# Stick-breaking attention's steps two units apart, and its sums in two rounded passes in layer 1

## The reference

```python
z = jnp.einsum('bhqd,bhkd->bhqk', qb, k).astype(jnp.float32) * scale
log_1mb = jnp.where(mask, jax.nn.log_sigmoid(-z), 0.0)
later = lax.cumsum(log_1mb, axis=3, reverse=True) - log_1mb
w = jnp.where(mask, jnp.exp(jax.nn.log_sigmoid(z) + later), 0.0)
return jnp.einsum('bhqk,bhkd->bhqd', w.astype(v.dtype), v)
```

## Time and profile before

| | |
|---|---|
| median of 3 runs | 1025.94 us (1024.55 to 1026.02) |
| the profiled execution | 1024.67 us, its span 1023.0 us |
| mean granted TensorE clock | 0.997 |
| TensorE matmuls | 985.5 us busy (96%) |
| VectorE | 764.5 us (75%) |
| ScalarE | 549.9 us (54%) |
| GpSimd | 47.3 us (5%) |
| HBM | 176.67 MB read, 176 GB/s over the span |

### The profile page before, as it was taken

The page is one execution under the profiler, slowest core; times in us unless marked ns, Lnnn a source line. Parts: engine busy times, 40 slices in busy tenths (PEclk is TensorE's granted clock), DMA queues, the critical chain, the costliest instruction groups (busy, mean ns, idle before and its releaser), DMA issues. The chain is left out here.

```text
span 1023.0 us, 17644 instructions
## 1 busy us (share of the span) xinstructions
PE 985.5 (96%) x6784; PEld 872.3 (85%) x6784; DVE 764.5 (75%) x1185; ACT 549.9 (54%) x843; POOL 47.3 (5%) x104
## 2 busy tenths in 40 slices
PE   6999999999999999999999999999999999999996
PEld 6877889999897888888889778999988878888885
DVE  5988997878765866879765669887887567656665
ACT  7455426475755645544463663545656565444543
POOL 5004000000000004000000110000000000000000
PEclk9999999999999999999999999999999999999999
DMA  9797438466654666686657853565565546666652
GB/s 339 230 191 179 125 103 268 147 168 184 181 148 124 244 189 183 190 228 187 191 145 206 169 156 104 151 196 152 179 182 168 141 128 188 194 191 188 186 187 80
DMA packets 64164, 181.37 MB, mean 177 GB/s; under 512 B 19729, under 2 KB 21777, under 8 KB 63441
## 3 DMA queue, kind: packets, MB, share of 16 engines
q1 hardware_dynamic: 63648, 179.91, 60.3%
q10 hardware_dynamic: 432, 0.32, 0.1%
HBM read 176.67 MB, written 3.54 MB: 176 GB/s over the span
## 5 line engine op out<-in xcount | busy, mean ns | idle before, releaser
L1289 DVE TENSOR_TENSOR s_w_lo<-s_raw,s_w_hi 128x1024 fp32r<-128x1024 f32 x312 | 374.1, 1227 | 95.6 <-ACT s_w_hi L914 92.0
L914 ACT ACTIVATE s_w_hi<-s_raw 128x1024 fp32r<-128x1024 f32 x312 | 320.1, 1054 | 180.2 <-PE p_T L1877 78.2
L1875 PE MATMUL p_T<-s_hT,s_w_hi 128*128 128x256 f32 x576 | 166.4, 289 | 1.5 <-ACT s_w_hi L914 1.5
L1876 PE MATMUL p_T<-s_hT,s_w_hi 128*128 128x256 f32 x576 | 163.4, 284 | 0.0
L1877 PE MATMUL p_T<-s_hT,s_w_lo 128*128 128x256 f32 x576 | 163.2, 283 | 0.0
L1875 PE MATMUL p_A<-s_w_hi,s_bT_hi 128*128 128x512 f32 x320 | 125.1, 391 | 2.5 <-DVE s_bT_lo L1289 2.5
L1877 PE MATMUL p_A<-s_w_hi,s_bT_lo 128*128 128x512 f32 x320 | 124.8, 390 | 0.0
L1876 PE MATMUL p_A<-s_w_lo,s_bT_hi 128*128 128x512 f32 x320 | 124.6, 389 | 0.0
L1875 PEld LDWEIGHTS p_T<-s_hT,s_w_hi 128*128 128x128 f32 x576 | 110.8, 192 | 5.5 <-issue 2.7
L1876 PEld LDWEIGHTS p_T<-s_hT,s_w_hi 128*128 128x128 f32 x576 | 110.9, 193 | 0.1
L1877 PEld LDWEIGHTS p_T<-s_hT,s_w_lo 128*128 128x128 f32 x576 | 110.9, 192 | 0.0
(11 more groups left out here) (269 smaller groups left out, 1826.6 us busy)
## 6 DMA issues: line engine op xcount, KB each, us to landing
s_raw<-in_weights SPq DMA_DIRECT2D x312, 512.0 KB, 3.7
s_bt<-in_ssm_bt SPq DMA_DIRECT2D x2, 1024.0 KB, 7.4
s_gates<-f_turn SPq DMA_DIRECT2D x16, 128.0 KB, 7.6
s_x<-in_x SPq DMA_DIRECT2D x1, 1024.0 KB, 10.1
s_dv<-in_ssm_bc SPq DMA_DIRECT2D x2, 512.0 KB, 8.9
u_turn<-s_st_y SPq DMA_DIRECT2D x4, 256.0 KB, 4.9
s_uB<-u_turn SPq DMA_DIRECT2D x16, 64.0 KB, 5.1
s_bt<-in_mem SPq DMA_DIRECT2D x1, 1024.0 KB, 7.1
```

The lines of the kernel that those rows point to most:

```text
L914: return nc.scalar.activation(o, i, f, **kw)
L1289: return V.tensor_tensor(o, i0, i1, op)
L1875: mm(o, lhi, rhi, start=first, stop=False, **kw)
L1876: mm(o, lhi, rlo, start=False, stop=False, **kw)
```

## The change

- Stick breaking's stages stand two units apart in both layers: sb_s at 6 + 2p, sb_u at 8 + 2p, sb_p at 10 + 2p. Its last ones are now at units 14 and 16.
- sb_u uses banks A0, A1 rather than X0, X1; ssm_in 0 and 1 use A2 and X0 rather than A1 and A0.
- The SSM in layer 1 starts at unit 13 as in layer 0; what counts from it (GELU, the transfers of y) moves along.
- In layer 1 `nl` is split into `nl_hi` (ScalarE, after a wait for the new signal nl_made) and `nl_lo` (VectorE, the new stage sb_l), which lie in the free rows of `gates`. TensorE multiplies both by rounded copies of `tri` and `ones`: four matmuls a head, of one pass each, instead of two in float32.
- In layer 1 VectorE puts `later` of sb_s (the addition into `nl`) between its two chunks, as it does for da_s.

```diff
-FIRST = [13, 12]
+FIRST = [13, 13]
...
     for p in range(SB_PAIRS):
         after(6 + 2 * p, "sb_s", p)
-        after(7 + 2 * p, "sb_u", p)
-        after(8 + 2 * p, "sb_p", p)
+        if l:
+            after(6 + 2 * p, "sb_l", p)
+        after(8 + 2 * p, "sb_u", p)
+        after(10 + 2 * p, "sb_p", p)
...
-        "mem_row": ["X0"], "sb_s": ["X0", "X1"], "sb_u": ["X0", "X1"], "sb_p": ["A3"], "turn": ["X0", "X1"],
+        "mem_row": ["X0"], "sb_s": ["X0", "X1"], "sb_u": ["A0", "A1"], "sb_p": ["A3"], "turn": ["X0", "X1"],
...
-        [["A1", "A0", "A1", "A1"][s[1]]] if s[0] == "ssm_in" else
+        [["A2", "X0", "A1", "A1"][s[1]]] if s[0] == "ssm_in" else
...
@@ ScalarE, later, sb_s
                         fn(nl, nl, ACT.Ln, bias=1.0).then_inc(*st.sig(ln_ready))
+                        if l:
+                            if s[1] == 0:
+                                fn(tri_r[:, :], tri[:, :]).then_inc(*st.mid())
+                                fn(ones_r[:, :], ones[:, :]).then_inc(*st.mid())
+                            act.wait_ge(*st.at(nl_made, s[1] + 1))
+                            fn(nl_hi, nl).then_inc(*st.sig(nl_split))
...
@@ VectorE, later
-                         .then_inc(*st.sig(nl_ready))
+                         .then_inc(*st.sig(nl_made if l else nl_ready))
...
+                    elif kind == "sb_l":
+                        dve.wait_ge(*st.at(nl_split, s[1] + 1))
+                        tt(nl_lo, nl, f32(nl_hi), ALU.subtract).then_inc(*st.sig(nl_ready))
...
-                    scores = [s for s in SIDES[l][u] if s[0] == "da_s"]
+                    scores = [s for s in SIDES[l][u] if s[0] == "da_s" or s[0] == "sb_s" and l]
...
@@ TensorE, sb_u
-                        for h, b in enumerate(("X0", "X1")):
+                        for h, b in enumerate(("A0", "A1")):
...
+                            if l:
+                                mm(o[:, 0:384], tri_r[:, :], nl_hi[:, h, :], start=True, stop=False)
+                                mm(o[:, 0:384], tri_r[:, :], nl_lo[:, h, :], start=False, stop=True)
+                                mm(o[:, P:T], ones_r[:, :], nl_hi[:, h, T:384], start=False, stop=False, skip_group_check=True)
+                                mm(o[:, P:T], ones_r[:, :], nl_lo[:, h, T:384], start=False, stop=True, skip_group_check=True)\
+                                    .then_inc(*st.sig(full[b]))
+                                continue
```

More of the change, by code:

```diff
@@ L244, in side_stages @@
     return side
-RANK = {"da_o": -1, "da_t": 1, "sb_p": 0, "da_p": 0, "sb_u": 1, "sb_s": 2, "da_s": 2, "da_c": 3, "da_n": 3,
+RANK = {"da_o": -1, "da_t": 1, "sb_p": 0, "da_p": 0, "sb_u": 1, "sb_s": 2, "sb_l": 2.5, "da_s": 2, "da_c": 3, "da_n": 3,
         "ssm_in": 4, "ssm_out": 6}
@@ L410, in hybrid_trunk @@
         bT_hi, bT_lo = sb("bT_hi", [P, 12, T], F32R), sb("bT_lo", [P, 12, T], F32R)
+        at = -(-nc.sbuf_base // 32) * 32 + 8 * T
         gates = sb("gates", [P, 16, T])
+        sums = nc.alloc_sbuf_tensor_at("s_sums", [P, 2, 768], F32R, offset=at)
+        tri_r, ones_r = sb("tri_r", [P, P], F32R), sb("ones_r", [P, P], F32R)
         qk = sb("qk", [P, KD, T])
@@ L474, in macc @@
             return dv[:, j, :] if cb == 0 else st_y[:, 0, 512 * j:512 * j + 512]
+        nl_hi, nl_lo = (sums[:, i, :].rearrange("p (h n) -> p h n", h=2) for i in range(2))
         eT_b = [att[:, 512 * i:512 * i + 512].rearrange("p (m n) -> p m n", m=2) for i in range(XA_HEADS)]
@@ L524, in hybrid_trunk @@
         ln_ready, nl_ready = signal("ln_ready", SB_PAIRS), signal("nl_ready", SB_PAIRS)
+        nl_made, nl_split = counted("nl_made", SB_PAIRS), counted("nl_split", SB_PAIRS)
         w_ready, sbp_done = signal("w_ready", SB_PAIRS), signal("sbp_done", SB_PAIRS)
@@ L1099, in stage @@
                         z = z_b[s[1] % 2]
-                        act.wait_ge(*st.at(*freed(l, "X0", s)))
-                        act.wait_ge(*st.at(*freed(l, "X1", s)))
+                        act.wait_ge(*st.at(*freed(l, "A0", s)))
+                        act.wait_ge(*st.at(*freed(l, "A1", s)))
                         fn(z, z, ACT.Exp).then_inc(*st.sig(w_ready))
```

## The result

| | before | after |
|---|---|---|
| median, 5 runs each | 1025.18 us (1024.55 to 1026.02) | 1030.02 us (1028.74 to 1031.49) |
| the profiled execution | 1024.67 us, span 1023.0 us | 1031.1 us, span 1029.3 us |
| mean granted TensorE clock | 0.997 | 0.995 |

The ratio is 1.0048, interval 1.0037 to 1.0060: slower by 4.8 us. 1028.4 was forecast, with 1024.5 to 1031.0 as the range. The sign, the place and most of the mechanism came as forecast.

A forecast was written before the change was run, and what follows sets the result against it. TensorE, busy 96% of the span, was taken as the bound, waiting for VectorE in the SSM stretch. Layer 0 and layer 1 with one clock fall gave 2.8 or 2.2, so +2.5 us: 1028.4 at the median, range 1024.5 to 1031.0.

The forecast's parts named there:

- Part 1, the rounded sums: Layer 1's cumulative sums on TensorE: 1.10 us a pair for 1.73, 2.5 us gained in four pairs unless a wait intervenes.
- Part 2, the waits for T0: Layer 1: ScalarE's nl_hi copy delays emptying T0; TensorE stalls 1.15, 1.2, 1.45 and 0.4 us, 4.2 in all.
- Part 3, layer 1: Later ssm steps on VectorE delay differential attention's turned weights; 1.7 us wait before da_t 0; layer +3.0 us.
- Part 3, layer 0: Moved stages: bt at 107.9, a 2.3 us wait at ssm_in 0, the 2.02 us wait before da_t 0 gone; -1.6 us.
- The clock: TensorE's clock falls after one of two waits, layer 0's 2.3 us or layer 1's 1.7; about 1.3 to 1.5 us lost.
- The forecast's second form: Clock falls at layer 1's wait only: layer 0 -1.6 us, layer 1 +3.8, together 2.2.
- T0 in time: Rival, layer 1: T0's copies finish without stalling TensorE; together -2.4 us, 1023.5 at the median; chance 0.14.
- Short tail: Rival: VectorE's tail in layer 1 shorter than layer 0's, da_t 0 wait mostly vanishes; +0.5 us, 1026.4; chance 0.14.
- Slow narrow products: Rival: narrow rounded matmuls take float32's passes, 0.10 us more each, 16 of them; +4.1 us, 1030.0; chance 0.06.

The follow-up runs named there:

- late_split: Changed kernel with ScalarE's copy of nl_hi and VectorE's remainder one unit later, behind ScalarE's copies of T0 and T1; 1026.25 us, ratio 1.0002.
- twice_inside: Changed kernel with VectorE's copy out of PSUM made twice in layer 1's gate units 14, 15 and 16, inside the ssm steps; 1034.15 us, ratio 1.0077.
- float_sums: Changed kernel with layer 1's sums back in float32, without nl_hi, nl_lo or the wait for nl_made; 1026.68 us, ratio 1.0012.
- l1_only: Changed kernel with layer 0's old stage spacing put back, layer 1 and the banks as changed; 1030.57 us, ratio 1.0045.
- mixed12: Layer 0 as before; layer 1's pairs 0 to 2 as in late_split, pair 3 in float32 at unit 13, SSM at unit 12; 1025.17 us, ratio 0.9998.
- fill: Changed kernel with ten unread 512-column matmuls put into layer 0's wait for bt; 1029.30 us, ratio 1.0033.
- l0_only: Changed kernel with layer 1 in its old spacing, in float32, SSM at unit 12; layer 0 and banks as changed; 1026.15 us, ratio 1.0003.
- late12: late_split with layer 1's SSM back at unit 12, everything else including the banks kept; 1032.21 us, ratio 1.0061.
- after_again: The changed kernel as it is, timed and profiled a second time; 1029.92 us, ratio 1.0040.
- twice_outside: Changed kernel with VectorE's copy out of PSUM made twice in layer 1's gate units 21, 22 and 23, behind the ssm steps; 1033.30 us, ratio 1.0073.

## Why the prediction was right, and where it was off

**Part 1, the rounded sums.** The narrow rounded matmul was taken at 0.10 us between 0.066 and 0.20. 384 columns are spaced by 0.17 to 0.18 (576.28, 576.46, 576.63), on the straight line. Of the two narrow ones the first is followed after 0.06 (576.63 to 576.69), the second after 0.11 (576.69 to 576.80): 0.085 each, between the straight line and the 0.10 taken. By the rule of the Trainium skill ("TensorE: Matmul & The Clock Gate", sections "LDWEIGHTS" and "Weight-path perf modes") the weights of 128 columns would have spaced them by 0.107. The trace agrees in part: the first spacing is well under that, but the weight loads of this pair come no closer than 0.11 (next fence).

```profile
576.63 0.19 PEld L2094 LDWEIGHTS p_A<-s_sums,s_ones_r 128*128 128x128 f32 x1
576.74 0.19 PEld L2091 LDWEIGHTS p_A<-s_sums,s_tri_r 128*128 128x128 f32 x1
576.85 0.19 PEld L2092 LDWEIGHTS p_A<-s_sums,s_tri_r 128*128 128x128 f32 x1
```

The pair took 1.19 us (576.28 to 577.47), and 1.29 in the other three, not 1.10: the second matmul of a head comes 0.06 to 0.12 later than the straight line (576.80 to 577.03), and a gap of 0.1 stands at the pair's end (577.26 to 577.47). So about 0.5 us was gained per pair for 0.63.

**Part 2, the waits for T0.** Forecast 1.15, 1.2, 1.45, 0.4; measured 1.09, 1.11, 1.29, 0.21, all four with the releaser named, 3.7 in all for 4.2. late_split shows that this is the cause of the loss: with `nl_hi` behind the copies they are gone and so are 3.8 us.

**Part 3, layer 1.** The wait before da_t 0 was 1.72 for a forecast of 1.7, and from VectorE's first ssm step to da_t 0 it was 31.84 us for 31.7; to da_t 1 another 8.32 for 8.3. The first ssm step came 0.37 us later than summed (97.93 us after the layer's start, 617.6 less 520.04 being 97.56); the three pairs ahead of it took 0.47 more, the waits for T0 0.3 less, and the rest wasn't followed. Layer 1 is +3.56 for +3.0. twice_inside confirms that VectorE's chain is the bound here, and float_sums the consequence that I hadn't drawn: I wrote that the 2.5 us of part 1 are gained unless a wait eats it, and a wait ate more than half of it. Without T0's stalls the rounded form is worth about 1 us by the traces.

**Part 3, layer 0: the step that failed.** I let bt come 1.4 us sooner, at 107.9, since the scores of pair 3 end sooner and VectorE wouldn't wait for ScalarE's copy. It came at 108.8. Counted from sb_s 0, to leave out the start's 0.35, that is 0.9 sooner. The scores themselves started 0.67 sooner by that count, for 0.8, and the minima can't start ahead of them: in after VectorE was ready and waited 0.23 for the scores. So the minima gained 1.0, not 1.4. Before (scores on TensorE, minima on VectorE):

```profile
99.88 0.70 PE L2065 MATMUL p_X<-s_qk 64*128 64x256 f32 x4
...
101.28 1.15 DVE L1289 TENSOR_TENSOR s_att<-p_X,s_masks 128x256 f32<-128x256 f32 x4
```

and after:

```profile
99.56 0.70 PE L2081 MATMUL p_X<-s_qk 64*128 64x256 f32 x4
...
100.61 1.15 DVE L1302 TENSOR_TENSOR s_att<-p_X,s_masks 128x256 f32<-128x256 f32 x4 [0.23 <-PE p_X L2083]
...
107.54 1.22 DVE L1302 TENSOR_TENSOR s_bt<-s_gates 128x1024 f32<-128x1024 f32 x1
```

The wait was 2.64 for 2.3. Then TensorE needed 35.85 us from ssm_in 0 to da_t 0 at full clock (float_sums, 109.05 to 144.90), where I had summed 35.56. The way from sb_s 0 to da_t 1 in layer 0, over all profiles:

| layer 0's stages | low clock in layer 0 | us |
|---|---|---|
| as before: before | 3.4 us, behind da_t 0 | 99.36 |
| as before: l1_only, mixed12 | none | 98.69, 98.66 |
| as after: float_sums, fill | none | 98.47, 98.45 |
| as after: l0_only, late_split, late12, after_again, twice_outside | 3.4 us, behind the wait for bt | 99.82 to 99.95 |
| as after: after, twice_inside | 7 us, behind the wait for bt | 101.21, 101.27 |

Against the profile of before, layer 0 is worth -0.9 without a fall and +0.5 to +0.6 with one of 3.4 us, where I had -1.6 and -0.2: the price of the fall, 1.4, was right, the term under it was 0.7 to 0.8 too good. With 7 us it is +1.9. And at equal clock the new order of layer 0 is worth only 0.2 us: 0.7 of the 0.9 is the fall that the profile of before had. l0_only, at 1.0003, puts layer 0 near nothing at the median.

**The clock.** One of two falls was held likeliest. In the first profile one came, at layer 0, longer than before's; in the second both did. A fall of 3.4 us behind da_t 0 costs 0.74 us (9.06 for 8.32), as forecast with 0.8. That the two executions differ in the length and number of falls, at equal waits, was not in my sum. I let before's wait of 2.02 us always bring its fall; in l1_only and mixed12 the same wait (2.03 and 2.02) brought none. And I held waits of 1.3 us for harmless; in l1_only and twice_outside the clock fell behind the one of 1.32 at layer 1's opening.

**The sum.** The forecast's second form was -1.6 for layer 0 and +3.8 for layer 1 with a fall, 2.2 together; 4.8 came. Measured one layer at a time at the median: +0.3 by l0_only (interval -0.6 to +1.1) and +4.6 by l1_only (3.4 to 5.8); by the trace, layer 1 is 3.56 and 0.74 for a fall, 4.3. So of the missing 2.6 us layer 1 has 0.5 to 0.8 and layer 0 about 1.9, of which 0.7 to 0.8 are the terms above; the rest hangs on which falls before and after had at the median, which one profile of each can't tell. The time lies well inside the range, the difference only just (4.8 for at most 5.1). That the time looks better is luck: before's median came out 0.8 lower in the five runs than in the three that I started from. The rival "T0 in time" gave 1023.5; late_split, which makes it true, was at 1026.25. Its layer 1 part was -0.71 (133.82 us to da_t 1 for 135.39, and ssm_out 3) against -0.8; what failed was again layer 0's -1.6. "Short tail" fell, since VectorE had no idle time of over 0.3 us between its ssm steps. "Slow narrow products" fell with 0.085 us each.

**Still open:** the 0.4 us behind da_t 1, half of what twice_outside costs at the median, and why a wait of 1.3 to 2.6 us lowers the clock in one execution and not in another.

## What to carry to other kernels

Before you put an instruction that waits into an engine's queue, list what stands behind it and when the next engine needs that: here 0.85 us of ScalarE work behind a wait of 0.7 to 1.1 us, four times over, cost 3.8 us, and one unit further on nothing that could be measured. A cheaper form on the engine that is busiest is worth only what the next hand-over lets through; look for the next wait on a second engine and shorten that first. An engine at 75% can be the bound at several short places, in and out of the stretch that you look at. And before you compare two profiles, count from an instruction that the change doesn't touch, and look for low clock on both sides: here 0.35 us of start and 0.7 us of before's low clock looked like an effect of the change.

## What the runs showed of the hardware

- **Equal waits, unequal clock.** After the wait of 2.6 us for bt the clock fell in seven profiles (after and after_again among them) and not in float_sums. After the wait of 1.7 to 2.0 us before da_t 0 it fell in before (layer 0), l1_only (layer 1), fill and after_again, and not in after, late_split and twice_outside, nor in layer 0 of l1_only and mixed12. After the 1.32 us at layer 1's opening it fell in l1_only and twice_outside, two of twelve. Waits of 3.9 us (twice_inside) and 6.3 us (late12) had it fall before they ended.
- **Unequal length.** A fall lasted about 3.4 us mostly, 7 us in after (layer 0) and twice in twice_inside, 10 us in late12, there with TensorE idle for the first half. In after TensorE was busy throughout (109 to 115: 1.00), and the clock stayed low all the same.
- **What a fall costs.** 3.4 us of low clock took 0.74 us behind da_t 0 and 1.4 us behind the wait for bt; 7 us took 2.0 (twice_inside, layer 1) and 2.7 (101.21 for 98.47).
- **Rounded float32, narrow.** 384 columns are spaced by 0.17 to 0.18 us, close to a straight line with 512 at 0.229; two matmuls of 128 columns took 0.17 together (0.06 and 0.11), and the weight loads around them came no closer than 0.11. In float32 a 128-column matmul is two instructions, and a head's 384 and 128 columns take 0.83 us together; the four rounded ones took 0.52 (576.28 to 576.80).
